# A hybrid attention and SSD layer on one core: all rows of x loaded at once, the v/dt products four tiles behind the transposes, two products of each pair exchanged, and the second block's first loads changed

## What is computed

```python
h = rms_norm(x, norm_gain)                      # x: (1, 1024, 1024) float32
proj = h @ w_in                                 # 1024 -> q k v z_a z_s xbc dt gates
q, k, v, z_a, z_s, xbc, dt_raw, gate_pre = split(proj)
o_a = window_attention(q, k, v, ...)            # 16 heads, 2 chunks of 64, rotary, sinks
branch_a = (o_a * silu(z_a)) @ w_attn_proj
y_s = ssd_mixer(xbc, dt_raw, ...)               # conv of width 4, silu, chunked scan, D skip
branch_b = rms_norm(y_s * silu(z_s)) @ w_ssd_proj
merged = sigmoid(g_a) * branch_a + sigmoid(g_b) * branch_b
out = x + merged @ w_out
```

## Time and profile before

| | |
|---|---|
| time, median of 3 runs | 1418.75 us (1415.56 to 1422.06) |
| time of the profiled execution | 1417.91 us |
| its span | 1416.1 us |
| PE busy | 1358.4 us (96%) |
| DVE, ACT, POOL busy | 782.6 (55%), 612.1 (43%), 585.1 (41%) |
| mean granted clock of TensorE | 0.986 |
| chain that ended last | PE 84%, issue 5%, POOL 3%, DVE 3%, DMA 2%, ACT 2% |
| first product starts | 68.94 us |
| last product of block 1 ends | 499.1 us |
| DVE per x tile: reciprocal, multiply, low subtraction | 0.16, 1.28, 1.22 us |
| loads of 1 MB into `wst` / of 1 MB rows in 512-byte pieces | 4.9 us / 6.9 us from issue to landing at the start of block 2 |

### The profile page before, as it was taken

One profiled execution on the slowest core, in us unless ns is written; L12 is line 12 of the kernel. 1 busy time (PEld: TensorE's weight loads), 2 busy tenths in 40 slices (PEclk: granted clock), 3 DMA queues, 4 the chain that ended last, 5 costly groups with the idle time before them and its releaser, 6 DMA issues.

```text
span 1416.1 us, 20612 instructions
## 1 busy us (share of the span) xinstructions
PE 1358.4 (96%) x7108; PEld 1088.0 (77%) x7108; DVE 782.6 (55%) x955; ACT 612.1 (43%) x1148; POOL 585.1 (41%) x344
## 2 busy tenths in 40 slices
PE   5698999999999979999999999999999999998999
PEld 4686777888888857888787878888768888776787
DVE  4775777676666455536554555555365554555311
ACT  5545444545444343435252535344356533323110
POOL 3443564445544423333333233333336666443321
PEclk9899999999999989999999999999999999999999
DMA  5331644422323276778666785869586265334431
GB/s 201 144 90 66 191 138 134 178 103 99 110 104 119 103 183 157 189 199 157 202 154 203 164 210 151 238 150 202 129 296 235 104 218 196 136 139 158 146 106 59
DMA packets 166500, 221.59 MB, mean 156 GB/s; under 512 B 7760, under 2 KB 127824, under 8 KB 166208
## 3 DMA queue, kind: packets, MB, share of 16 engines
q1 hardware_dynamic: 130640, 172.64, 43.0%
q10 hardware_dynamic: 35728, 48.37, 9.4%
q0 software_dynamic: 96, 0.13, 0.0%
HBM read 152.57 MB, written 63.31 MB: 152 GB/s over the span
## 4 chain that ended last, share of the span: by engine, by line
PE 84%; issue 5%; POOL 3%; DVE 3%; DMA 2%; ACT 2%; SPq 0%; ACTq 0%; POOLq 0%; DVEq 0%
PE F L180 37%; PE F L930 28%; PE F L1772 3%; PE M L1772 3%; PE M L1093 2%; PE M L1136 2%; DMA sb_early<-x_d 2%; POOL sb_res L1596 1%; PE F L1130 1%; PE F L1123 1%; PE F L1107 1%; PE M L1130 1%; PE M L1123 1%; PE F L1725 1%; PE F L899 1%
## 5 line engine op out<-in xcount | busy, mean ns | idle before, releaser
L180 PE MATMUL F<-sb_xb,sb_whl 128*128 128x512 f32 x1536 | 376.3, 402 | 0.0
L180 PEld LDWEIGHTS F<-sb_xb,sb_whl 128*128 128x128 f32 x1536 | 286.9, 188 | 75.2 <-issue 9.2
L192 POOL TENSOR_TENSOR sb_whl<-sb_wst,sb_whl 128x1024 fp32r<-128x1024 f32 x64 | 159.3, 2490 | 405.6 <-ACT sb_whl L189 405.3
L180 PE MATMUL F<-sb_X,sb_whl 128*128 128x512 f32 x1104 | 259.7, 396 | 5.9 <-issue 3.0
L180 PEld LDWEIGHTS F<-sb_X,sb_whl 128*128 128x128 f32 x1104 | 206.5, 187 | 58.5 <-issue 8.2
L930 PE MATMUL F<-sb_tv,sb_whl 128*128 128x512 f32 x1008 | 242.4, 396 | 2.3 <-DVE sb_acc L734 2.3
L930 PEld LDWEIGHTS F<-sb_tv,sb_whl 128*128 128x128 f32 x1008 | 189.2, 188 | 49.3 <-issue 3.1
L414 POOL TENSOR_TENSOR sb_whl<-sb_acc,sb_whl 128x512 fp32r<-128x512 f32 x103 | 145.7, 1421 | 135.8 <-ACT sb_whl L461 135.8
L930 PE MATMUL F<-sb_xb,sb_whl 128*128 128x512 f32 x756 | 187.6, 401 | 7.5 <-POOL sb_whl L414 5.7
L930 PEld LDWEIGHTS F<-sb_xb,sb_whl 128*128 128x128 f32 x756 | 142.7, 190 | 46.3 <-POOL sb_whl L414 7.6
L189 ACT ACTIVATE sb_whl<-sb_wst 128x1024 fp32r<-128x1024 f32 x64 | 67.6, 1058 | 198.4 <-DMA sb_wst<-w_units 97.1
(11 more groups left out here) (216 smaller groups left out, 1776.5 us busy)
## 6 DMA issues: line engine op xcount, KB each, us to landing
sb_wst<-w_units SPq DMA_DIRECT2D x64, 512.0 KB, 5.8
sb_acc<-cs_d SPq DMA_DIRECT2D x8, 2048.0 KB, 20.6
sb_wst<-w_units SPq DMA_DIRECT2D x12, 1024.0 KB, 4.9
x_d<-sb_res ACTq DMA_DIRECT2D x24, 512.0 KB, 2.7
...
```

Source lines behind the costliest of these rows:

```text
L180: last = nc.tensor.matmul(bank, weight(slot, wp, k), act(ap, k, half), start=(k == 0 and wp == 0 and ap == 0), stop=(k == NK - 1 and wp == 1))
L192: return nc.gpsimd.tensor_tensor(weights(slot, 1), raw_unit(slot), weights(slot, 0).bitcast(f32), ALU.subtract)
```

## The change

- x: the rows of a tile go to their own place in `early` (the room of X1, in 512-byte pieces), all loads are issued without a wait; tile 0, then the v and dt weights, then tiles 1 to 7.
- `ttmp` has two buffers, and `sums` a place of its own.
- v/dt: PE runs `project_vdt(n - 4)` instead of `n - 1` behind the transposes of tile n; ACT and DVE run `v_copy(n - 5)` and `take_dt(n - 5)`; the last ones stand behind the loop. The low part of dt's weights goes from POOL to DVE.
- Products 4 and 5 of a pair exchange places with their banks, weights and takes; `c11` waits for the sixth product, `take_c21` for the fifth. ACT splits the next pair's first two operands before `c11`.
- Block 2: SP's first loads wait for the fifth product of the last pair; `bc` is issued before `csb`; `state` is cleared by POOL, and PE waits for it only before `off(0)`; PE's start waits for `u2_done` instead of `c12_done`; ACT's first unit split waits for one product less.

```diff
...
-        xrow, w = carve(acc_all, 2 * NK * VD, 3, DM)
+        ttmp2, w = carve(acc_all, 2 * NK * VD, 4, 4, P)
+        sums, w = carve(acc_all, w, 2, HALF)
         cst1, w = carve(acc_all, w, NCONST - BLOCK1_CONSTS)
...
         gqs, w = carve(acc_all, w, 2, T)
-        sums, _ = carve(acc_all, 2 * NK * VD + 2 * DM, 2, HALF)
-        ttmp, _ = carve(part_all, 0, 4, 4, P)
+        ttmp1, _ = carve(part_all, 0, 4, 4, P)
+        ttmp = (ttmp1, ttmp2)
         zpad, _ = carve(part_all, 0, 256)
...
         raw_in = sems("raw_in0", "raw_in1")
-        x_in = sems("x_in0", "x_in1", "x_in2")
+        x_in = sems("x_in0", "x_in1", "x_in23", "x_in45", "x_in67")
         stored = sems("stored0", "stored1")
...
         SLOT = (0, 1, 2, 3, 0, 1, 2)
-        BANK = (0, 1, 2, 3, 0, 2, 3)
+        BANK = (0, 1, 2, 3, 2, 0, 3)
         kinds = [kind for kind, _ in PAIRS]
...
+        def xrow(n):
+
+            rows = early.rearrange("p a (s k t) -> p (a s) k t", s=2, k=NK)
+            return rows[:, n % 4, :, (2 + n // 4) * P:(3 + n // 4) * P]
+
         def t_block(part_, q, lo=0, hi=4):
...
-            tv, blk = ((None, 0), (2, None), (3, None), (0, None), (None, 2), (1, None), (None, 3))[idx]
+            tv, blk = ((None, 0), (2, None), (3, None), (0, None), (1, None), (None, 2), (None, 3))[idx]
             return XB[:, blk, ap, k, :] if tv is None else TV[:, tv, ap, k, :]
...
-            return (raw_w(n, 0, 0), sums[:, 1, :], raw_w(n, 1, 0), sums[:, 0, :], raw_w(n, 0, 1), raw_w(n, 1, 1), sums[:, 1, :])[idx]
+            return (raw_w(n, 0, 0), sums[:, 1, :], raw_w(n, 1, 0), sums[:, 0, :], raw_w(n, 1, 1), raw_w(n, 0, 1), sums[:, 1, :])[idx]
...
             def load_x(n):
-                sp.dma_start(xrow[:, n % 3, :], a["x"][TILES[n] * P:(TILES[n] + 1) * P, :]).then_inc(x_in[n % 3], 16)
+                sp.dma_start(xrow(n), a["x"][TILES[n] * P:(TILES[n] + 1) * P, :].rearrange("t (k c) -> t k c", c=P)).then_inc(x_in[n if n < 2 else n // 2 + 1], 16)
...
             load_x(0)
-            load_x(1)
             sp.dma_start(wst[:].rearrange("p (a c) -> p a c", a=2), a["w_units"][V0:V0 + 2].rearrange("a p c -> p a c")).then_inc(v_in1, 16)
             sp.dma_start(dtraw[:], a["w_units"][0].rearrange("p (k c) -> p k c", k=NK)[:, :, 0:NHS]).then_inc(v_in1, 16)
-            load_x(2)
-            for n in range(3, NT):
-                sp.wait_ge(xt_done, n - 2)
+            load_x(1)
+            for n in range(2, NT):
                 load_x(n)
-                if n == 4:
-                    sp.wait_ge(v_lo, 3)
-                    load_raw(0)
+            sp.wait_ge(v_lo, 2)
+            load_raw(0)
             sp.wait_ge(x_lo, NT)
...
                       raw_unit(u).rearrange("p (k c) -> p k c", k=NK))
-            v_low(2, vw[:, 0, :, 2 * P:VD], vw[:, 1, :, 2 * P:VD], dtraw[:])
             pool.wait_ge(pads_set, 2)
...
                 n = 4 if q < 3 else 2
-                nc.gpsimd.tensor_tensor(t_block(1, q, 0, n), ttmp[:, 0:n], t_block(0, q, 0, n).bitcast(f32), ALU.subtract).then_inc(t_lo, 1)
+                nc.gpsimd.tensor_tensor(t_block(1, q, 0, n), ttmp[q % 2][:, 0:n], t_block(0, q, 0, n).bitcast(f32), ALU.subtract).then_inc(t_lo, 1)
             for n in range(NPAIR):
...
             def b12_copy(q):
-                if q:
-                    act.wait_ge(t_lo, q)
-                else:
+                if q >= 2:
+                    act.wait_ge(t_lo, q - 1)
+                elif q == 0:
                     act.wait_ge(pads_in, 48)
-                nc.scalar.activation(ttmp[:, 3].rearrange("p k t -> p (k t)"), x_banks(2 * q + 1)[:, 0, :], ACT.Copy).then_inc(b12_copied, 1)
+                nc.scalar.activation(ttmp[q % 2][:, 3].rearrange("p k t -> p (k t)"), x_banks(2 * q + 1)[:, 0, :], ACT.Copy).then_inc(b12_copied, 1)
...
                 act.wait_ge(t_done, q + 1)
-                nc.scalar.activation(t_block(0, q), ttmp[:], ACT.Copy).then_inc(t_hi, 1)
+                nc.scalar.activation(t_block(0, q), ttmp[q % 2][:], ACT.Copy).then_inc(t_hi, 1)
...
-            for n in range(NT):
-                act.wait_ge(x_in[n % 3], 16 * (n // 3 + 1))
-                nc.scalar.activation(whl[:, 3 * DM:4 * DM], xrow[:, n % 3, :], ACT.Square, accum_out=ssx[:, 0, n:n + 1]).then_inc(x_sq, 1)
+            def square_x(n):
+                if n < 2:
+                    act.wait_ge(x_in[n], 16)
+                else:
+                    act.wait_ge(x_in[n // 2 + 1], 32)
+                nc.scalar.activation(whl[:, 3 * DM:4 * DM].rearrange("p (k c) -> p k c", c=P), xrow(n), ACT.Square,
+                                     accum_out=ssx[:, 0, n:n + 1]).then_inc(x_sq, 1)
                 act.wait_ge(x_sq, n + 1)
                 nc.scalar.activation(ssx[:, 0, n:n + 1], ssx[:, 0, n:n + 1], ACT.Sqrt, bias=eps[:], scale=1.0 / DM).then_inc(x_rt, 1)
+
+            def v_high(u):
+                act.wait_ge(v_in1, 32)
+                nc.scalar.activation(vw[:, 0, :, u * P:(u + 1) * P], raw_unit(u).rearrange("p (k c) -> p k c", k=NK),
+                                     ACT.Copy).then_inc(v_hi, 1)
+
+            for n in range(NT):
                 if n == 1:
-                    act.wait_ge(v_in1, 32)
-                    for u in range(2):
-                        nc.scalar.activation(vw[:, 0, :, u * P:(u + 1) * P], raw_unit(u).rearrange("p (k c) -> p k c", k=NK),
-                                             ACT.Copy).then_inc(v_hi, 1)
+                    v_high(0)
+                square_x(n)
+                if n == 1:
+                    v_high(1)
                     nc.scalar.activation(vw[:, 0, :, 2 * P:VD], dtraw[:], ACT.Copy).then_inc(v_hi, 1)
...
                     t_high((n - 3) // 2)
-                if n >= 3:
-                    v_copy(n - 3)
+                if n >= 5:
+                    v_copy(n - 5)
             x_high(NT - 1)
...
             split(0, 0)
-            v_copy(NT - 3)
+            for n in range(NT - 5, NT - 2):
+                v_copy(n)
             t_high(3)
...
                 kind, m = kinds[n], before_pair(kinds[n], n)
-                act.wait_ge(prod, 7 * n + 5)
+                act.wait_ge(prod, 7 * n + 6)
                 free_raw_a(n)
...
                     nc.scalar.activation(ssq_sb[:], M[:, 0, :], ACT.Copy).then_inc(ssq_copied, 1)
+                if n + 1 < NPAIR:
+                    split(n + 1, 0)
+                    split(n + 1, 1)
                 c11(n)
...
                     act.dma_start(ecs_d[:, :], csT[:, :]).then_inc(cs_stored, 16)
-                if n + 1 < NPAIR:
-                    split(n + 1, 0)
-                    split(n + 1, 1)
             post_b(NPAIR - 1)
             post_a(NPAIR - 1)
+            act.wait_ge(prod, 7 * NPAIR - 1)
+            high(act, 0, 0, 0)
             act.wait_ge(prod, 7 * NPAIR)
-            high(act, 0, 0, 0)
             high(act, 1, 0, 0)
...
                 def tmp(v):
-                    return ttmp[:, v].rearrange("p k t -> p (k t)")
+                    return ttmp[q % 2][:, v].rearrange("p k t -> p (k t)")
...
                 ch.link(nc.vector.reciprocal(ssx[:, 1, n:n + 1], ssx[:, 0, n:n + 1]))
-                nc.vector.scalar_tensor_tensor(xrow[:, n % 3, :], xrow[:, n % 3, :], ssx[:, 1, n:n + 1], gain[:],
+                nc.vector.scalar_tensor_tensor(xrow(n), xrow(n), ssx[:, 1, n:n + 1], gain[:].rearrange("p (k c) -> p k c", c=P),
                                                ALU.mult, ALU.mult).then_inc(xn_ready, 1)
+                if n == 2:
+                    dve.wait_ge(v_hi, 3)
+                    nc.vector.tensor_tensor(vw[:, 1, :, 2 * P:VD], dtraw[:], vw[:, 0, :, 2 * P:VD].bitcast(f32),
+                                            ALU.subtract).then_inc(dt_lo, 1)
                 if n >= 1:
...
                     dve.wait_ge(block1_in, 16)
-                if n >= 3:
-                    take_dt(n - 3)
+                if n >= 5:
+                    take_dt(n - 5)
             x_low(NT - 1)
-            take_dt(NT - 3)
+            for n in range(NT - 5, NT - 2):
+                take_dt(n)
             combine_x(3)
...
             dve.wait_ge(t_hi, 4)
-            nc.vector.tensor_tensor(t_block(1, 3, 2, 4), ttmp[:, 2:4], t_block(0, 3, 2, 4).bitcast(f32), ALU.subtract).then_inc(t_lo2, 1)
+            nc.vector.tensor_tensor(t_block(1, 3, 2, 4), ttmp[1][:, 2:4], t_block(0, 3, 2, 4).bitcast(f32), ALU.subtract).then_inc(t_lo2, 1)
             take_dt(NT - 1)
...
             def take_c21(n):
-                dve.wait_ge(prod, 7 * n + 6)
+                dve.wait_ge(prod, 7 * n + 5)
                 nc.vector.tensor_tensor(raw[:, 1, 0:HALF], u2[:], F[:, 2, :], ALU.add).then_inc(c21_done, 1)
...
                     last = nc.tensor.transpose(x_banks(n)[:, k // 4, (k % 4) * P:(k % 4 + 1) * P],
-                                               xrow[:, n % 3, k * P:(k + 1) * P], C("ident"))
+                                               xrow(n)[:, k, :], C("ident"))
```

(29 more changed lines are left out.)

6 lines of the change are left out of this document (3 added, 3 removed).

## The result

The changed kernel takes 1454.05 us (median of 4 runs, 1452.76 to 1457.56), the kernel before 1418.83 in the same comparison: a ratio of 1.0252, 95% interval 1.0223 to 1.0282. It is slower, as forecast, but by 35 us where 16 were forecast, and outside my range (1421 to 1446).

A forecast was written before the change was run, and what follows sets the result against it. PE, busy 96% of the span, was taken as the bound, so only its idle places count. Terms 1.0 + 13.4 + 8.5 - 6.0 = +16.9 us on 1417.91 gave 1434.8, stated as 1435; range 1421 to 1446.

The forecast's parts named there:

- First stage: Work up to the first product: +1.0 us (-7 to +3), first product at 70.0 against 68.94.
- The clock term: At the first product: the clock falls as before after about 3 us idle, 0; if it holds, -2.5 to -3.
- Order of products: Block 1 pairs: the exchanged fifth product must wait for DVE's third take (u3), +13.4 us (+9 to +18).
- the alternation of 0.2 and 1.3: Pairs 4 to 7: u3 alone delays the fifth product by 0.2, 1.3, 0.2 and 1.3 us, 3.0 in all.
- the high end: Upper bound of the order of products, +18: a further POOL hold of about 1.2 us in each of four pairs.
- The clock: PE's longer idles in the pairs drop its clock to the lower level: +8.5 us (0 to +14).
- Block 2: The second block: no wait for bc, heads' transposes at 531.7 instead of 537.68, -6.0 us (-8 to -3).
- the later pairs of block 2 suffer: Rival, chance 0.13: in iterations 2 to 8 the third weight unit comes about 4 us later; +14, 1449 us.
- it decides from 6 us: Same rival in block 2: the third weight unit's delay matters only from 6 us, by PE's need at 628.1.

The follow-up runs named there:

- a_comb_early: Changed kernel with the last combination and its copy moved ahead of two v/dt copies: 1446.70 us, ratio 1.0213.
- a_u3_early: Changed kernel with only DVE's program changed, so that u3 stands ahead of the rotary and reciprocal work it followed: 1428.45 us, ratio 1.0062.
- b_new_order: Kernel before with only the exchange of products 4 and 5 and ACT's splits ahead of `c11`: 1441.55 us, ratio 1.0163.
- a_old_order: Changed kernel with the order of products, their waits and the splits as before: 1428.33 us, ratio 1.0062.
- b_split_only: Kernel before with only ACT's two splits for the next pair moved ahead of `c11`: 1420.00 us, ratio 1.0008.
- b_bc_first: Kernel before with only `bc` issued ahead of `csb` in block 2: 1423.22 us, median of 10, ratio 1.0034.
- a_cs_first: Changed kernel with `csb` issued ahead of `bc` in block 2 again, as before: 1441.97 us, ratio 1.0161.

## Why the prediction was wrong in size, point by point

**First stage: +1.0 forecast, +0.7 measured; right.** The last transposes came at 48.33 (forecast 49 to 50), the last v/dt product ended near 65.4 (forecast 66.9), the first product came at 69.60 (forecast 70.0) after 4.18 us of idle. The reason I gave, the copies of the late v/dt products ahead of the combination, is the one that a_comb_early removes; I had not seen that moving two copies would keep the gain. The clock term was 0, with -2.5 to -3 if it held; it was -1.0, as the first product was fast in part.

**Order of products: +13.4 forecast, +15.9 measured; right.** Pair 1 +2.8 (forecast 3.1), pair 2 +3.0 net of the 0.95 that went (2.8), q pairs 4 x 2.52 = 10.1 (7.4). In the q pairs the slip was of one size, not the alternation of 0.2 and 1.3 that I carried over the earlier trace rows. In pair 4 SP issued the swap transfers 0.9 us later against PE's products (I had 1.1), and two of DVE's rotary steps took 2.23 and 2.22 us instead of 1.31 and 1.72, the kind of surcharge that I had only at the high end; that POOL's splits beside them are the reason was not tried. That DVE's program order is the cause is shown by a_u3_early, and that nothing else of the change is needed for it by b_new_order.

**The clock: +8.5 forecast, +10.4 measured; right within its bounds.** Falls behind 4.13 and 5.79 us, as forecast (2.4 and 2.2). Of the four idles of 2.5 us I counted one; behind all four the clock fell (1.5, 2.4, 1.6, 1.3). That the clock stays after 1.81 us, which I read from rows 4, was the luck of one execution: the same idle in pair 2 was followed by 4.19, 4.24 and 4.58 us for 12 matmuls in a_old_order, b_split_only and b_bc_first. The run without an idle fits too: in a_comb_early the first 12 matmuls took 2.96 us instead of 4.45. The rule of the Trainium skill ("TensorE: Matmul & The Clock Gate", What's actually happening) that the lower level is the default and activity releases it was the one that spoke against this change, and the traces bear it out.

**Block 2: -6.0 forecast, +12.3 measured; here it failed.** The first iteration went as described, only weaker. PE's start is 1.5 us later (I had put this at 0, inside the wait that follows); from its start to the heads' transposes it is 30.1 us instead of 35.5, so 5.4 shorter (forecast 6.0). The wait left there is 4.21 us, where I had 2, and the clock falls behind it (8 transposes take 1.97 us instead of 1.09). Later in the same iteration 1.7 us go in the wait for L1280.

The step that failed is a term that I put at nothing: the iterations behind the first. I had looked at them, as the rival "the later pairs of block 2 suffer", with a chance of 0.13. Its first half was right: "about 4 us" later for the third weight unit, against 3.8 to 6.1 measured in tiles 2 to 8, counted from PE's matmuls. Its second half, "it decides from 6 us", was wrong. I read this cover from PE's own need of the unit, which was met. I did not follow the unit through POOL's program, where it holds the decay of the state and so DVE's `add_state` and `weights_T`. On that road the cover was 5.8 us in the second tile of the kernel before (the first L1258 ends near 628.1, PE's products come at 633.92), and 1.7 of it went because L1280 now ran beside POOL's split. So about 4 us of delay were enough, and PE waited 8.6 us for L1280.

Nor did I ask what the exchange does to transfers that SP does not issue: the store of y landed 14.5 us later, and by POOL's product and DVE's L1271 PE waited 5.2 us. The right price was 11.5 us for six iterations on the profiled execution, close to the +14 of that rival and in part by its cause. That the exchange of the two issues is the cause is shown by b_bc_first and a_cs_first; the roads in between are read from the traces. Why the store of y lands later was not tried.

**What it comes to.** On the profiled execution: 0.7 + 15.9 + 10.4 + 12.3 = 39.3 of 39.7, where I summed 16.9. Of the 22.4 us that I was short, 18.3 are block 2. The measured 1454 us is beyond the forecast and its range because two cases that I treated as alternatives, my forecast and that rival, came together.
